# Norms computed in the stages before them: a two-block transformer step in fp32 on one core, its layers written out

## The chip, the core and the metric

The kernel runs on one core of a Trainium2 chip. A core has five engines that run their own instruction streams and meet through semaphores: TensorE (PE, matmul, with PEld for its weight loads), VectorE (DVE), ScalarE (ACT), GpSimd (POOL), and SyncE (SP), which here issues the DMAs. The metric is the device time of one execution in microseconds. One measurement of this kernel can tell about 0.2% from no change.

## The reference

256 rows of width 1024, in fp32, pass through two blocks. Cut to what matters:

```python
def first_block(x, ...):
    for layer in range(2):
        h = rmsnorm(x, g_mix); proj = h @ w_in            # 1024 x 7,756 columns
        y = sum over 3 branches of sigmoid(gate_b) * (attention_b(proj) @ w_branch[b])
        x = x + y @ w_out
        x = x + square(relu(rmsnorm(x, g_mlp) @ w_up)) @ w_down   # 1024 x 4096 and back
    return rmsnorm(x, g_final)

def second_block(x, ...):
    x = layer_norm(ALPHA * x + gated_deltanet(x), g00, b00)
    x = layer_norm(ALPHA * x + (silu(x @ w_gate) * (x @ w_up)) @ w_down, g01, b01)   # width 2816
    x = layer_norm(ALPHA * x + swa_sink_attention(x), g10, b10)
    x = layer_norm(ALPHA * x + moe_swiglu(x), g11, b11)           # 8 experts of width 3584, top 2
```

Every norm needs the mean and the variance of whole rows of x, so it cannot be finished before the last sum of the stage ahead of it.

## The kernel before

**Stages.** The kernel is a chain of stages. Each stage is one `nc.Block()`: at its end all five engines meet at a barrier, SP too. The rows of x lie in SBUF as two groups of 128 partitions (t = 0, 1), 1024 wide; a matmul needs them transposed (xT: 8 chunks of 128 partitions, 256 columns).

**Norms.** `norm_stage` is a stage of its own. DVE takes the sums of squares (`bn_stats`, two per t), a few operations on single columns and a reciprocal, ACT takes the square root, DVE scales the rows (a `tensor_scalar`, L367 or L369). PE transposes them (L397, 16 transposes into four PSUM banks), and ACT (L341, L343) and DVE (L379, L381) bring the banks to xT, multiplied by a gain (and shifted) by columns. Where the second block needs the normed x itself (final, ln00, ln01), POOL and DVE also multiply the rows with gains broadcast to all partitions (L314, L319); for ln10 this stands in the routing stage (L2463, L2465).

**Split stages.** Most products are done in three passes. ACT rounds the weights to fp32r (the "high" part), DVE subtracts to get "low", both for x (`xh`, `xl`) and for the weights, and PE sums xh·high, xl·high, xh·low. `split_projection_stage` (L550), `output_stage` (L1298) and `mlp_stage` (L1432, L1442) work so. They begin by rounding all of xT and the first two units of weights; a unit is a quarter or a half of a 2 MB tile. `projection_stage`, used for swa_proj alone, is plain fp32 (L436, L445).

**Weights.** SP loads tiles of 2 MB into a ring of six places (`Weights.load`, L198). `fill` loads the first tiles of a plan, after that each tile given free is loaded again (`load_behind`). The two layers of the first block are one body in a `Fori` loop, with a plan of its own each round; the first two tiles are loaded in the norm stage at the loop's head, the other four in a_proj. Between the layers `tidy` clears all semaphores in a stage of its own.

**Order.** First block, per layer: mix_norm, a_proj, stick-breaking attention, a_turn, bc_proj, the other branches, gates, y_turn, mix_out, mlp_norm, mlp, tidy. Second block: final norm, gdn_proj, gated delta stages, gdn_turn, gdn_out, tidy, ln00, ffn, ln01, swa_proj, sliding-window attention, swa_turn, swa_out, ln10, route, the experts (L2652, L2658; their weights pass through a ring of 1 MB places), last norm. y_turn, gdn_turn and swa_turn are stages that transpose y into xT before an output stage (L647, copies L604).

Of the kernel before, what the change touches and what calls it, by code (L numbers as in the profile page):

```python
# [64 lines left out]
BUCKETS, MAX_DIST = 32, 128  # L65
FFN_DIM, EXPERT_DIM, E = 2816, 3584, 8
# [44 lines left out]
class Core:  # L111


    def __init__(self, nc, ctx):
# [6 lines left out]
        self.scope, self.sems = ctx, []  # L121
        self.arenas = []
# [14 lines left out]
    @contextmanager  # L137
    def scratch(self, name, size=ARENA, start=0):

        outer = self.arenas  # L140
        with self.nc.sbuf_tensor(f"{name}_arena", [P, size], F32) as arena:
            self.arenas = outer + [(start, arena[:])]
            yield
        self.arenas = outer

    def sem(self, name):
        s = self.scope.enter_context(self.nc.semaphore(name))
        self.sems.append(s)
        return s

    @contextmanager
    def semaphores(self):

        outer, self.sems = (self.scope, self.sems), []
        with ExitStack() as self.scope:
            yield self.sems
        self.scope, self.sems = outer
# [22 lines left out]
class Weights:  # L180
# [3 lines left out]
    def __init__(self, core, tag, slots, plan):  # L184
        self.core, self.slots, self.plan = core, slots, plan
# [22 lines left out]
    def refill(self, sp, first, last):  # L208

        for n in range(first, last):  # L210
            if n + self.slots < len(self.plan):
                sp.wait_ge(self.tile_used, n + 1)
                self.load(sp, n + self.slots)

# [48 lines left out]
class Affine:  # L263
# [3 lines left out]
    NAMES = ("final", "ln00", "ln01", "ln10", "ln11")  # L267

    def __init__(self, core, a):
        self.core = core  # L270
        self.gain = core.sbuf("gain_columns", [P, len(self.NAMES), KC])
        self.shift = core.sbuf("shift_columns", [P, len(self.NAMES), KC])
        self.rows = core.sbuf("affine_rows", [P, 2, D])
        self.fetched = core.sem("affine_fetched")
        self.count = 0
        ln = [(a["ln_g_2"][i, j], a["ln_b_2"][i, j]) for i in range(2) for j in range(2)]
        self.sources = dict(zip(self.NAMES, [(a["g_final"], None)] + ln))

    def load_columns(self, sp, a, loaded):

        sp.dma_start(self.gain[:, 0, :], a["g_final"].rearrange("(p k) -> p k", k=KC)).then_inc(loaded, 16)
        for dst, name in ((self.gain, "ln_g_2"), (self.shift, "ln_b_2")):
            sp.dma_start(dst[:, 1:5, :], a[name].rearrange("i j (p k) -> p (i j) k", k=KC)).then_inc(loaded, 16)

    def fetch(self, sp, name):
        for i, source in enumerate(self.sources[name]):
            if source is not None:
                sp.dma_start(self.rows[:, i, :], row_broadcast(source)).then_inc(self.fetched, 16)
                self.count += 16


def norm_stage(core, tag, eps, gain, shift=None, natural=False, before=None, pool_first=None,
               vectors=None, y=None):

    nc = core.nc
    at = 0
    if y is None:  # L300
        y, at = core.part(0, NT, D)
    stats, at = core.part(at, NT, 12)
    mv, at = core.part(at, NT, 2)
    rstd, at = core.part(at, NT, 1)
    warm, at = core.part(at, 1)
    x = core.x
    rms = shift is None
    s = {n: core.sem(f"{tag}_{n}") for n in ("squares", "mean_square", "variance", "root", "inverse", "normed", "turned", "gained0", "gained1")}

    def natural_tile(eng, t):  # L310

        eng.wait_ge(core.affine.fetched, core.affine.count)
        eng.wait_ge(s["normed"], NT)
        op = eng.tensor_tensor(x[:, t, :], y[:, t, :], core.affine.rows[:, 0, :], ALU.mult)  # L314
        if not rms:
            gained = s[f"gained{t}"]
            op.then_inc(gained, 1)
            eng.wait_ge(gained, 1)
            eng.tensor_tensor(x[:, t, :], x[:, t, :], core.affine.rows[:, 1, :], ALU.add)  # L319

    with nc.Block() as block:
        @block.sync
        def _(sp):
            if before is not None:
                before(sp)

# [2645 lines left out]
```

## Time and profile before

| what | us |
|---|---|
| three runs | 2879.19, 2880.88, 2884.61 |
| median | 2880.88 |
| profiled execution: its own time | 2890.15 |
| span of its trace | 2888.4 |
| PE busy | 2598.8 (90%) |
| DVE busy | 1758.3 (61%) |
| ACT busy | 1350.9 (47%) |
| POOL busy | 110.8 (4%) |

The profile has one execution. Its windows view gives each engine's busy time in a stretch, with the clock granted to TensorE as a share of 2.4 GHz and the share of the DMA engines in use. Its waits view sums the idle time of an engine by what ended it. Its timeline lists instructions by start; a row's bracket holds the idle time ahead of it and what ended it.

### The profile page before, as it was taken

The numbers are of one execution on the slowest core, as the hardware profiler recorded it, in microseconds if no ns is written. First come the engines' busy times: TensorE is split into PE (matmuls) and PEld (weight loads), VectorE is DVE, ScalarE is ACT, GpSimd is POOL, SyncE is SP. The second block draws the span as 40 slices with busy tenths as digits, with TensorE's granted clock in tenths as the row PEclk, the third lists the DMA queues.
The fourth block names the chain that finished last, engine by engine and source line by source line (L and its number), as shares of the span: only waits on it lengthen the run. The fifth ranks groups of instructions, "written<-read, shape, count | busy, mean of one in ns | idle before, by whom it ended". The sixth has DMA issues, their size and how long they took to land. (4 is left out here: it accounts for less than half of the span.)

```text
span 2888.4 us, 34560 instructions
## 1 busy us (share of the span) xinstructions
PE 2598.8 (90%) x13577; PEld 2128.4 (74%) x13577; DVE 1758.3 (61%) x2037; ACT 1350.9 (47%) x1480; POOL 110.8 (4%) x155
## 2 busy tenths in 40 slices
PE   5999979978989799876879988799999999999996
PEld 5675469976744699746769977688887888888885
DVE  4334355543342555565554434688888988888897
ACT  3631234436312344321233413477777777777775
POOL 0100000001001000003200000000000000000000
PEclk9988989989899899887989995799999999999998
DMA  8141335162413351640055540499999999999996
GB/s 306 63 147 59 110 123 199 65 235 73 164 65 111 137 184 59 238 52 4 2 186 194 180 120 1 159 366 364 362 345 363 355 340 356 359 358 344 362 357 231
DMA packets 392739, 584.57 MB, mean 202 GB/s; under 512 B 22848, under 2 KB 286336, under 8 KB 392448
## 3 DMA queue, kind: packets, MB, share of 16 engines
q1 hardware_dynamic: 392576, 582.33, 59.3%
q8 instruction: 110, 1.80, 0.3%
q14 instruction: 53, 0.43, 0.0%
HBM read 578.09 MB, written 4.19 MB: 202 GB/s over the span
## 5 line engine op out<-in xcount | busy, mean ns | idle before, releaser
L2757 DVE TENSOR_TENSOR moe_low<-ring,moe_high 128x2048 fp32r<-128x2048 f32 x288 | 658.4, 2290 | 106.9 <-ACT moe_high L2721 101.8
L2721 ACT CAST moe_high<-ring 128x2048 fp32r<-128x2048 f32 x288 | 549.3, 1907 | 169.0 <-PE bank L2658 88.6
L2652 PE MATMUL bank<-moe_high,moe_xh 128*128 128x512 f32 x896 | 240.8, 391 | 7.9 <-PEq L2470 7.9
L2652 PE MATMUL bank<-moe_high,moe_xl 128*128 128x512 f32 x896 | 240.5, 391 | 0.0
L2652 PE MATMUL bank<-moe_low,moe_xh 128*128 128x512 f32 x896 | 240.2, 390 | 0.0
L2652 PEld LDWEIGHTS bank<-moe_high,moe_xh 128*128 128x128 f32 x896 | 168.7, 188 | 43.0 <-issue 8.1
L2652 PEld LDWEIGHTS bank<-moe_high,moe_xl 128*128 128x128 f32 x896 | 168.9, 188 | 35.0
L2652 PEld LDWEIGHTS bank<-moe_low,moe_xh 128*128 128x128 f32 x896 | 168.6, 188 | 34.9
L2658 PE MATMUL bank<-moe_high,moe_hh 128*128 128x512 f32 x448 | 128.1, 408 | 15.5 <-DVE moe_hl L2762 8.1
L1486 DVE TENSOR_TENSOR mlp_low<-upper_ring,mlp_high 128x2048 fp32r<-128x2048 f32 x36 | 82.5, 2293 | 95.5 <-ACT mlp_high L1457 95.5
L1457 ACT CAST mlp_high<-upper_ring 128x2048 fp32r<-128x2048 f32 x36 | 68.7, 1908 | 114.7 <-PE bank L1432 58.7
L2757 DVE TENSOR_TENSOR moe_low<-xT,moe_high 128x2048 fp32r<-128x2048 f32 x48 | 110.0, 2292 | 20.1 <-ACT moe_high L2721 19.0
L2658 PE MATMUL bank<-moe_high,moe_hl 128*128 128x512 f32 x448 | 121.4, 393 | 0.0
L2658 PE MATMUL bank<-moe_low,moe_hh 128*128 128x512 f32 x448 | 119.9, 390 | 0.0
L2721 ACT CAST moe_high<-xT 128x2048 fp32r<-128x2048 f32 x48 | 91.7, 1910 | 33.5 <-PE bank L2652 18.0
L689 PE MATMUL bank<-upper_ring,xT 128*128 128x512 f32 x192 | 104.5, 678 | 3.0 <-DVE lower_arena L701 3.0
L1486 DVE TENSOR_TENSOR mlp_low<-ring,mlp_high 128x2048 fp32r<-128x2048 f32 x28 | 64.0, 2292 | 68.7 <-ACT mlp_high L1457 68.7
L2658 PEld LDWEIGHTS bank<-moe_high,moe_hl 128*128 128x128 f32 x448 | 84.8, 189 | 19.3
L2658 PEld LDWEIGHTS bank<-moe_high,moe_hh 128*128 128x128 f32 x448 | 77.6, 191 | 28.3 <-ACT moe_high L2721 17.2
L2658 PEld LDWEIGHTS bank<-moe_low,moe_hh 128*128 128x128 f32 x448 | 84.3, 188 | 17.7
L689 PE MATMUL bank<-ring,xT 128*128 128x512 f32 x192 | 91.7, 622 | 2.1 <-PEq L638 2.1
L1457 ACT CAST mlp_high<-ring 128x2048 fp32r<-128x2048 f32 x28 | 53.1, 1903 | 80.0 <-PE bank L1432 57.7
(566 smaller groups left out, 4905.7 us busy)
## 6 DMA issues: line engine op xcount, KB each, us to landing
ring<-in_moe_w_gate SPq DMA_DIRECT2D x206, 512.0 KB, 5.1
ring<-in_moe_w_up SPq DMA_DIRECT2D x206, 512.0 KB, 6.5
ring<-in_moe_w_down SPq DMA_DIRECT2D x88, 1024.0 KB, 6.9
ring<-in_w_in SPq DMA_DIRECT2D x18, 2048.0 KB, 9.3
xT<-in_moe_w_down SPq DMA_DIRECT2D x25, 1024.0 KB, 7.0
upper_ring<-in_w_in SPq DMA_DIRECT2D x10, 2048.0 KB, 14.0
upper_ring<-in_w_up SPq DMA_DIRECT2D x10, 2048.0 KB, 8.2
upper_ring<-in_w_down SPq DMA_DIRECT2D x8, 2048.0 KB, 7.7
```

The costliest lines, as they stand in the source:

```text
L689: mm = pe.matmul(self.core.banks[6 + t][:], self.core.xT[:, c, t * P:(t + 1) * P], self.w.tile(self.first + j, KC, BW)[:, c, :], start=(c ...
L1457: act.copy(unit(high, u), raw(u)).then_inc(s["weight_high"], 1)
L1486: dve.tensor_tensor(unit(low, u), raw(u), unit(high, u), ALU.subtract)\
L2652: mm = pe.matmul(core.banks[i % 2][:], (xl if other_low else xh)[:, place(m), 4 * part + c, :], wt[:, c, :], start=(part == 0 and j == 0 a ...
L2658: mm = pe.matmul(core.banks[4 + half][:], (hl if other_low else hh)[:, i % 2, c, :], wt[:, c, half * BANK:(half + 1) * BANK], start=(own = ...
L2721: act.copy(unit(high, u), ring.raw(u)).then_inc(s["weight_high"], 1)
L2757: dve.tensor_tensor(unit(low, u), ring.raw(u), unit(high, u), ALU.subtract)\
```

## The change

- A norm is no longer a stage. `Norm` (a class) puts it at the end of the stage whose sums it takes: DVE adds a bank into x and takes its squares at once (`last_sums`), the t = 0 rows as soon as their last matmul is done (`first_sum`), the scaling writes the normed rows with the gain in one operation (two for a layer norm), and PE transposes them in the same block (`turn_rows`). Only the very first norm keeps a stage.
- ACT rounds the first two weight units of the next stage in that tail (`behind`, with a `Lead`).
- The next stage takes x from the PSUM banks: `Turned.high` (ACT, 512 columns each) and `Turned.low` (DVE) round from the bank. xT is written only for bc_proj and the routing (`keep`).
- Gains and shifts are rows of all partitions, fetched by SP for the next norm once the current one is done (`Norm.fetch`); their column forms and their loads at the start are gone.
- y_turn, gdn_turn and swa_turn now lie in their output stages; swa_proj is a split stage, except for the 128 columns of V.
- The layers are written out, one plan of tiles covers both, and the plan of gdn follows it. The stages of `tidy` between them are gone; POOL clears semaphores in later stages.
- The first norm stage loads six tiles (`w.fill`), not two.
- In the first unit of a stage the pass xh·low comes ahead of xl·high.
- The routing stage no longer computes rows of x; the sixth place of the experts' ring is loaded earlier, in the output stage.

```diff
-def norm_stage(core, tag, eps, gain, shift=None, natural=False, before=None, pool_first=None,
-               vectors=None, y=None):
...
+    def last_sums(self, dve, unit_used, first_units, units, first_sum, bank):
+
+        dve.wait_ge(unit_used, first_units)
+        for t in range(NT):
+            self.add(dve, t, 0, bank(t, 0))
+
+        def first():
+            dve.wait_ge(first_sum, 1)
+            return self.add(dve, 0, 1, bank(0, 1))
+
+        def second():
+            dve.wait_ge(unit_used, units)
+            return self.add(dve, 1, 1, bank(1, 1))
+        self.halves(dve, first, second)
...
+    def behind(self, act, unit_used, units, lead):
+
+        if lead is not None:
+            act.wait_ge(unit_used, units - 1)
+            lead.high(act, 0)
+            if lead.halves:
+                lead.high(act, 1)
+        self.roots(act)
+        if lead is not None and not lead.halves:
+            act.wait_ge(unit_used, units)
+            lead.high(act, 1)
...
+    def fetch(self, sp):
+        if self.following is not None:
+            sp.wait_ge(self.s["normed"], NT)
+            self.core.affine.fetch(sp, self.following)
...
+def norm_stage(core, norm, lead, before):
...
+        def _(sp):
+            before(sp)
+            norm.fetch(sp)
...
-        norm_stage(core, "mix_norm", RMS_EPS, core.layer_vectors[:, 0, 0:KC], before=lambda sp: w.fill(sp, 0, 2),
...
-            (2, "N", BW, keep_N(core, v))], before=lambda sp: w.fill(sp, 2))
...
+                    norm_stage(core, norm, lead, w.fill)
...
-                with nc.Fori(0, DEPTH) as i:
...
-    projection_stage(core, "swa_proj", w, [(first, "T", BW, with_bias(qT, bq, 0, HD ** -0.5)),
```

`Turned.high` and `Turned.low`, and the split swa_proj:

```python
    def high(self, act, b):
        act.wait_ge(self.turned, b + 1)
        act.copy(self.part(self.core.xh, b), self.banks[b][:]).then_inc(self.x_high, 1)

    def low(self, dve, b):
        dve.wait_ge(self.x_high, b + 1)
        dve.tensor_tensor(self.part(self.core.xl, b), self.banks[b][:], self.part(self.core.xh, b), ALU.subtract)\
           .then_inc(self.x_low, 1)
...
    split_projection_stage(core, "a_proj", w, [(first, "T", BW, with_bias(qT, bq, 0, HD ** -0.5)),
                                                 (first + 1, "T", BW, with_bias(qT, bq, 4, HD ** -0.5)),
                                                 (first + 2, "KV", 3 * P, keep_kv)], x, 4,
                           before=lambda sp: core.band.fetch(sp, bias))
```

**DVE at the end of mix_out in the first layer.** Before, the last add is followed by a barrier (the branch at L346 waits for it), then come the statistics of both t, then the scaling of both, and after the transposes the copies of xT and the rounding.

```order
L1328 TENSOR_TENSOR x<-bank,x 128x512 [waits mix_out_unit_used]
L1328 TENSOR_TENSOR x<-bank,x 128x512
L1261 UNCONDITIONAL_BRANCH
L346 UNCONDITIONAL_BRANCH [waits barrier_Pool_Activation_PE_DVE_SP_release]
L350 BN_STATS mlp_norm_arena<-x 128x6 x2
L353 BN_AGGR mlp_norm_arena<-mlp_norm_arena 128x2 [waits mlp_norm_squares]
L358 SCALAR_TENSOR_TENSOR mlp_norm_arena<-mlp_norm_arena 128x1 [waits mlp_norm_squares]
L361 TENSOR_SCALAR mlp_norm_arena<-mlp_norm_arena 128x1 [waits mlp_norm_mean_square]
L350 BN_STATS mlp_norm_arena<-x 128x6 x2
```

After, at the same place:

```order
L638 TENSOR_TENSOR x<-bank,x 128x512 [waits mix_out_first_sum]
L436 BN_STATS norm_small<-x 128x6 [waits mlp_norm_step]
L447 BN_AGGR norm_small<-norm_small 128x2 [waits mlp_norm_step]
L451 SCALAR_TENSOR_TENSOR norm_small<-norm_small 128x1 [waits mlp_norm_step]
L453 TENSOR_SCALAR norm_small<-norm_small 128x1 [waits mlp_norm_step]
L473 RECIPROCAL norm_small<-norm_small 128x1 [waits mlp_norm_root,affine_fetched]
L478 SCALAR_TENSOR_TENSOR xT<-x,norm_small,affine_rows 128x1024 [waits mlp_norm_step]
L638 TENSOR_TENSOR x<-bank,x 128x512 [waits mix_out_unit_used]
L436 BN_STATS norm_small<-x 128x6 [waits mlp_norm_step]
```

The rows of t = 0 are scaled ahead of the last add of t = 1; no barrier stands between add and norm.

**SP at the first norm of the program.** Before, two tiles are issued in the norm's block and the rest in a_proj's.

```order
L198 DMA ring<-in_w_in 128x8x512
L198 ISA
L198 DMA ring<-in_w_in 128x8x512
L321 UNCONDITIONAL_BRANCH
L506 UNCONDITIONAL_BRANCH [waits barrier_Pool_Activation_PE_DVE_SP_release]
L198 ISA
L198 DMA ring<-in_w_in 128x8x512
```

After:

```order
L530 UNCONDITIONAL_BRANCH [waits barrier_Pool_Activation_PE_DVE_SP_release]
L241 DMA ring<-in_w_in 128x8x512 x3
L241 DMA upper_ring<-in_w_in 128x8x512 x3
L336 DMA affine_rows<-in_g_mlp 128x1024 [waits mix_norm_normed]
L529 UNCONDITIONAL_BRANCH
L705 UNCONDITIONAL_BRANCH [waits barrier_Pool_Activation_PE_DVE_SP_release]
```

Six tiles and a gain row now stand ahead of the barrier that opens a_proj (L705).

## Rows read from the trace of the kernel before

**Rows 1.** Windows: stretch; PE, PEld, DVE, ACT, POOL busy (count); PEclk, DMA share, GB/s

```profile
402.00:414.00 12.00, 3.68 (x16) 3.28 (x16) 9.33 (x21) 5.89 (x11) 0.00 (x0) 0.58 0.00 1
...
1735.00:1797.00 62.00, 58.59 (x247) 47.26 (x245) 25.51 (x117) 23.60 (x99) 0.00 (x0) 0.58 0.00 1
...
2400.00:2870.00 470.00, 456.75 (x2100) 377.23 (x2099) 414.13 (x299) 339.02 (x283) 0.00 (x0) 1.00 1.02 349
```

**Rows 2.** Waits of PE in the experts, longest sum: total us, times, longest

```profile
PE bank L2658 <- DVE moe_hl L2762: 8.1, 4, 2.0
```

**Rows 3.** Timeline, mix_out to mlp, first layer: start, length, instruction, [idle before]

```profile
398.82 1.07 PE L1298 MATMUL bank<-mix_out_low,mix_out_xh 128*128 128x512 f32 x4
399.93 1.29 DVE L1328 TENSOR_TENSOR x<-bank,x 128x512 f32<-128x512 f32 x2 [5.45 <-PE bank L1298]
...
404.71 0.21 DVE L353 BATCH_NORM_AGGREGATE mlp_norm_arena<-mlp_norm_arena 128x2 f32<-128x12 f32 x1
...
405.48 0.75 DVE L367 TENSOR_SCALAR mlp_norm_arena<-x,mlp_norm_arena 128x1024 f32<-128x1024 f32 x1
...
414.05 2.08 PE L1432 MATMUL bank<-mlp_xh,mlp_high 128*128 128x256 f32 x8 [4.09 <-ACT mlp_high L1457]
...
420.48 1.12 PE L1432 MATMUL bank<-mlp_xh,mlp_low 128*128 128x256 f32 x8
...
421.44 1.12 PE L1432 MATMUL bank<-mlp_xh,mlp_high 128*128 128x256 f32 x8
```

**Rows 4.** Timeline, end of the first layer to a_proj of the second

```profile
595.38 1.29 DVE L1328 TENSOR_TENSOR x<-bank,x 128x512 f32<-128x512 f32 x2 [4.15 <-PE bank L1442]
...
603.16 1.29 DVE L350 BATCH_NORM_STATS2 lower_arena<-x 128x6 f32<-128x512 f32 x2 [6.49 <-issue]
...
614.84 1.50 PE L550 MATMUL bank<-a_proj_xh,a_proj_high 128*128 128x256 f32 x8 [3.24 <-ACT a_proj_high L585]
```

**Rows 5.** Timeline, second mlp to gdn_proj, with the load of a gain row

```profile
1168.80 1.29 DVE L1328 TENSOR_TENSOR x<-bank,x 128x512 f32<-128x512 f32 x2 [4.15 <-PE bank L1442]
...
1186.44 2.08 PE L550 MATMUL bank<-gdn_proj_xh,gdn_proj_high 128*128 128x256 f32 x8 [4.37 <-ACT gdn_proj_high L585]
...
1193.90 5.25 SPq L288 DMA_DIRECT2D affine_rows<-in_ln_g  x1
```

**Rows 6.** Timeline, gdn_out to ffn

```profile
1472.02 1.28 DVE L1329 SCALAR_TENSOR_TENSOR x<-x,bank 128x512 f32<-128x512 f32 x2 [5.45 <-PE bank L1298]
...
1493.47 2.08 PE L1432 MATMUL bank<-ffn_xh,ffn_high 128*128 128x256 f32 x8 [7.63 <-ACT ffn_high L1457]
```

**Rows 7.** Timeline, ffn to swa_proj

```profile
1684.45 1.29 DVE L1329 SCALAR_TENSOR_TENSOR x<-x,bank 128x512 f32<-128x512 f32 x2 [1.43 <-PE bank L1442]
...
1698.79 30.64 PE L445 MATMUL bank<-xT,upper_ring 128*128 128x256 f32 x128 [4.76 <-PEq L321]
...
1729.26 7.07 PE L445 MATMUL bank<-xT,ring 128*128 128x256 f32 x32
```

**Rows 8.** Timeline, gate to mix_out in the first layer

```profile
368.78 0.69 DVE L1229 TENSOR_TENSOR lower_arena<-bank,lower_arena 128x512 f32<-128x512 f32 x1 [2.74 <-PE bank L1202]
...
369.55 1.26 POOL L1240 TENSOR_TENSOR upper_bc_arena<-upper_bc_arena,lower_arena 128x512 f32<-128x512 f32 x1 [2.17 <-DVE lower_arena L1229]
...
371.89 0.59 ACT L604 COPY xT<-bank 128x512 f32<-128x512 f32 x1 [38.47 <-PE bank L647]
...
376.25 1.73 PE L1298 MATMUL bank<-mix_out_high,mix_out_xh 128*128 128x512 f32 x4 [3.06 <-ACT mix_out_high L1283]
```

**Rows 9.** Timeline, last norm: scaling with a row of gains

```profile
2880.04 1.28 DVE L2824 SCALAR_TENSOR_TENSOR last_arena<-x,last_arena,affine_rows 128x1024 f32<-128x1024 f32 x1
```

**Rows 10.** Timeline, start: SP issues of tiles, and a_proj's second group

```profile
20.04 10.16 SPq L198 DMA_DIRECT2D ring<-in_w_in  x3
...
30.39 8.60 SPq L198 DMA_DIRECT2D upper_ring<-in_w_in  x3
...
36.04 1.12 PE L550 MATMUL bank<-a_proj_xh,a_proj_high 128*128 128x256 f32 x8
```

More of the change, by code:

```diff
@@ L279, in load_columns @@
[L279 to L283, printed above, removed]
+        self.sources = {}
+        for i in range(DEPTH):
+            self.sources[f"mix{i}"] = (a["g_mix"][i],)
+            self.sources[f"mlp{i}"] = (a["g_mlp"][i],)
@@ L292, in norm_stage @@
-def norm_stage(core, tag, eps, gain, shift=None, natural=False, before=None, pool_first=None,
-               vectors=None, y=None):
-    nc = core.nc
[L299 to L319, printed above, removed]
+            sp.dma_start(self.rows[:, i, :], row_broadcast(source)).then_inc(self.fetched, 16)
@@ new lines, in wait, with clear, __init__, high @@
+    def wait(self, eng, name):
+        eng.wait_ge(self.fetched, self.there[name])
+def clear(pool, sems):
+    for s in sems:
+        pool.sem_clear(s)
+class Lead:
+    def __init__(self, core, w, tile, raw, halves):
+        self.core, self.w, self.tile, self.raw, self.halves = core, w, tile, raw, halves
+    def high(self, act, u):
+        self.w.wait(act, self.tile)
+        act.copy(self.core.unit(self.core.high, u, self.raw(u), self.halves), self.raw(u))
+def mlp_lead(core, w, first):
+    return Lead(core, w, first, lambda u: w.tile(first, KC, BW)[:, :, u * 2 * P:(u + 1) * 2 * P], False)
@@ new lines, in norm_stage, with _, all_squares @@
+def norm_stage(core, norm, lead, before):
+    with core.nc.Block() as block:
+        @block.sync
+        def _(sp):
+            before(sp)
+            norm.fetch(sp)
+        @block.vector
+        def _(dve):
+            def all_squares(t):
+                norm.squares(dve, t, 0)
+                return norm.squares(dve, t, 1)
+            norm.halves(dve, lambda: all_squares(0), lambda: all_squares(1))
+        @block.scalar
+        def _(act):
+            norm.roots(act)
+            for u in range(2):
+                lead.high(act, u)
+        @block.tensor
+        def _(pe):
+            norm.turn_rows(pe)
@@ L2905, in first_half, with second_block, clear_between, fill_free @@
+def second_block(core, a, r, ring, gdn, results, lower, between):
+    mid = Weights(core, "mid", SLOTS, mid_plan(a))
+    swa_first = 2 * (FFN_DIM // FB)
+    raw, z, ba = results
+    def clear_between(pool):
+        clear(pool, between)
+    with core.semaphores() as of_gdn:
         with core.scratch("gdn_upper", GDN_UPPER, GDN_LOWER), \
                 core.nc.sbuf_tensor("gdn_more", [P, SLOT], F32) as more:
-            gdn_stages(core, a, gdn, raw, z, ba, more[:])
-    def fill_free(sp):
-        for n in range(SLOTS):
-            if n not in (1, 2):
+            gdn_stages(core, a, gdn, raw, z, ba, more[:], clear_between)
+        lower.close()
+        def fill_free(sp):
+            for n in (0, 3, 4, 5):
```

928 lines of the change are left out of this document (486 added, 442 removed).

## The prediction

> **What bounds the kernel now.** I read the page's shares first, then the windows view by stage, then the timeline around every stage boundary. TensorE (PE) is busy for nine tenths of the span, and in the experts for 457 of 470 us, at full clock and with the DMA engines full [rows 1]; its longest wait there sums to 8 us [rows 2]. The change does not touch the experts, which are a third of the span, so I cost them at nothing: they are bound by PE and by weights together. What can be won lies at the boundaries. There PE has little: of the 12 us between mix_out and mlp it is busy for 3.7, and its clock falls to 0.58 of 2.4 GHz, nearly the 1.2 GHz level [rows 1]. So the view to read is the timeline from the last matmul of a stage (T0) to the first matmul of the next.
>
> **Five norm boundaries before.** With T0 as the start of the last adds, the first matmul of the next stage starts at T0 + 14.1 for mlp (399.93 to 414.05, [rows 3]; the second layer repeats it), T0 + 19.5 from the first layer to the second (595.38 to 614.84, [rows 4]), T0 + 17.6 into gdn_proj [rows 5], T0 + 21.4 into ffn [rows 6] and T0 + 14.3 into swa_proj [rows 7]. That is six places in all. The layer boundary is longer because a stage of its own clears semaphores: the norm's statistics start 6.5 us after the adds [rows 4].
>
> **The tail, step by step.** After the change t = 0 gets its last sum 12 matmuls early. Four take 0.91 us at full clock (a group of four is listed with 1.07, its end is modelled [rows 3]), so the chain of t = 0 starts at T0 - 2.7. It is: one add 0.65 and one bn_stats 0.65 (halves of the x2 rows [rows 3, 4]), five small operations of about 0.2 (the L353 row, [rows 3]) with their hand-over, 1.1 together, then the scaling. The old scaling took 0.75 [rows 3]. The new one also reads a row of gains, as L2824 does, so I take 1.28 [rows 9]. That ends at T0 + 1.0. Then t = 1: add 0.65, bn_stats 0.65, small operations 1.1, scaling 1.28: normed at about T0 + 4.7. Half of the 16 transposes are left by then, about 2.3 us with their hand-over, and the barrier takes 0.3: the next block starts at T0 + 7.3. Its first matmul needs one 512-column rounding by ACT, for which I take the 0.59 of the bank copy [rows 8]: **T0 + 8.0**. Weights are rounded by then, in ACT's idle time. A layer norm has a second two-tensor operation for each t, some of it behind waits: 2.1 more, T0 + 10.1.
>
> The scaling is the one place where the new form of an operation is dearer, and the rows show it: 1.28 for two tensors against 0.75 for one. The Trainium skill (VectorE: DVE Perf Modes, Mode 2×_2P — use both read ports for one tensor) says why: a one-tensor operation can use both read ports, a two-tensor one cannot, since the second port carries the other tensor; the trace agrees. Priced by the old row, the tail would be 1.1 us shorter at each of six places.
>
> **What each boundary gives at an unchanged clock:** mlp twice, 14.1 - 8.0 = 6.1 each; second layer 19.5 - 8.0 = 11.5; gdn_proj 17.6 - 8.0 = 9.6; ffn 21.4 - 10.1 = 11.3; swa_proj 14.3 - 10.1 = 4.2. From each I take 1.5 for the clock. PE comes back after a rest with a group of eight at 2.08 instead of 1.12 [rows 3], some 1 us lost in a group; after the change it has its transposes and then passes that wait for roundings one bank at a time, so I expect one or two such groups more. The bounds are 0 and 3. This leaves 9.2 + 10.0 + 8.1 + 9.8 + 2.7 = **39.8**.
>
> **swa_proj as a split stage.** A plain fp32 matmul has two records, so the 32 records in 7.07 us are 16 matmuls of 0.44 [rows 7]. In three passes the starts of groups of eight are 0.96 apart [rows 3], 0.36 for the same product. There are 80 such products (ten blocks of 128 columns, eight chunks): 0.08 x 80 = **6** saved, if ACT and DVE keep up; 0 if they don't. Each has one operation of 1024 columns in a block, no longer than the 1.28 of [rows 9], against PE's 2.9. A sentence of the Trainium skill would give more: by FP8 and Floating Point Precision, TensorE Precision Notes, true fp32 is four passes, so three would save a quarter, 8.8 us; the rows give 6, and the sum goes by them.
>
> **Turns inside the output stages.** Before, from the last gate operation to mix_out's first matmul are 7.5 us [rows 8]. What has to stay is POOL's 1.26 [rows 8] after DVE's 0.69, the first transposes of a bank (0.4 to 1) and one rounding from the bank 0.59. The copies to xT, a barrier, and the wait for the weight rounding (ACT 1.90 at L1283 in the block, now done while PE turns) go. I take 3.5, bounds 2 and 5: 7 for two layers. gdn_out and swa_out have the same pattern without POOL: 3.5 each, **14** in all. The routing stage starts its logits sooner by the shorter norm but copies xT first, and no longer computes rows of x: 2, bounds 0 and 6, since a choice of experts and the gather follow serially.
>
> **What it costs: the first norm.** Before, the block of the first norm issues two tiles. Now it issues six and then a row, and the barrier waits for SP. The trace has what six issues take: the issues end at 30.2 for the first three and at 39.0 for the next three [rows 10], although each needs only about 0.5 when the queue is empty. They are held, as the row load at 1193.90 is, which takes 5.25 behind six tiles [rows 5]. The start stage issues five column loads less (0.5 to 1.0 us each, some 3 together, in the timeline's first 6 us), so all this comes up to 3 earlier. SP leaves the block at 39.0 - 3 + 0.4 to 5.3, in the middle 39, and a_proj's second group, at 36.0 before [rows 10], comes about 6.5 later than 39: 45.5. I take **-10**; bounds -14, and +3 if the issues do not hold the block. Behind SP stand all five engines; nobody has other work there. At the other tails the row is issued with a slot or two of the ring outstanding and I cost it at nothing: mlp uses up 16 tiles in the 181 us from 414.05 to 595.38 [rows 3, 4], 11.3 each, and a tile of 2.1 MB lands in 6 at the 349 GB/s of [rows 1], so the queue is empty; if it is not, each costs up to 3, since the transposes cover about 2 of 5.25.
>
> **Sum.** 39.8 + 6 + 14 + 2 - 10 = 51.8. The profiled execution took 2890.15 (span 2888.4), which gives 2838; it lies 9.3 above the median. From the median 2880.88 the forecast is 2829.
>
> **Rivals.**
> (1) SP does not hold the first block. For it: one issue alone is short. Against it: rows 10 at that very place. It gives 13 more: 2816.
> (2) The clock stays up. PE's rest shrinks from 14 to 8 us, with transposes inside. Then the 1.5 at six places come back, and as much at the four output stages' starts at most 3: 9 to 12, 2818. Against it: 0.58 in a 12-us stretch [rows 1]. With (1) too, 2806.
> (3) A row load is held at every tail. For it: 5.25 at 1193.90 [rows 5]. Against it: there six tiles stood ahead. Six places x 3 = 18: 2847.
> (4) Slower than before: the clock stays near its lower level well into each stage. For it: from 1735 to 1797 PE is busy for 58.6 of 62 us and the granted clock is still 0.58 [rows 1], so being busy is not enough. Its place is the first units after six norms; a group of eight then costs 0.96 more (2.08 against 1.12, [rows 3]). It decides from 52 + 6 = 58 us more, that is ten such groups more at each of six places; it gives 2887. Against it: in mlp the second unit runs at 1.12 already, 7 us after the first matmul.
> (5) Half of the tail's gain is lost, because DVE and ACT are late with low parts: the first unit's time grows by what its start gains. 2849.
>
> **Chances.** Forecast 0.47, (1) 0.15, (2) 0.14, both 0.05, (3) 0.08, (5) 0.07, (4) 0.03, and 0.01 that it is within 0.2%. Over 0.2% is about what a measurement of this kernel can tell from no change. Faster by over 0.2% is 0.96, the same 0.01, slower 0.03. The range from 2808 to 2846 holds the forecast with its bounds, (1) and (2), and leaves out both together, (3) to (5): about 0.2.
>
> **What would show it.** The first matmul after a norm at T0 + 8 to 9 (RMS) and 10 to 11 (layer norm); scalings of 1.28; a_proj starting near 40 with SP's row load as the last thing ahead of the barrier; ten blocks of swa_proj 2.9 us apart; mix_out's first matmul 4 us after the last gate operation; the experts unchanged at some 1005 us. The forecast is wrong if the clock in the windows after the boundaries is lower than before for longer than 3 us, if a row load takes over 2 us at the tails, or if a_proj starts near 30.

## The result and the profile after

Four executions of the changed kernel took 2831.16 to 2843.19 us, median 2837.64; the kernel before, on the same chip, 2882.74 (2879.19 to 2895.30). The ratio is 0.9833, 95% interval 0.9808 to 0.9857: by the ratio 48 us faster, 41 to 55. The forecast was 52 us less, 2829 by the median of before then shown, range 2808 to 2846. Of the profiled executions it said 2838; the changed kernel's took 2839.29 (span 2837.5, before 2888.4).

The page of the changed kernel: engine, busy us (share of the span), instructions. PE works nearly as long as before (2598.8), so the 51 us that the span lost are idle time.

```profile
PE 2597.4 (92%) x13657; PEld 2120.2 (75%) x13657; DVE 1751.7 (62%) x2022; ACT 1363.3 (48%) x1501; POOL 93.3 (3%) x146
```

Where it went is read from the timelines: for each stage, the time from the first matmul of one to the first of the next, in both profiles. Every number in this table is a difference of two starts of PE rows, except that the last row ends with the end of the last matmul. The decay sums are the first matmuls of the second attention branch, behind bc_proj (L994 before, L1213 after).

| from first matmul to first matmul | before | after | gain |
|---|---|---|---|
| start of the span to a_proj, first layer | 31.6 | 44.2 | -12.7 |
| to the first layer's decay sums | 161.5 | 162.7 | -1.2 |
| decay sums to gates, first layer | 132.7 | 136.1 | -3.4 |
| gates to mix_out, first / second layer | 50.4 / 50.5 | 48.0 / 47.9 | 2.5 / 2.5 |
| mix_out to mlp | 37.8 / 37.8 | 30.9 / 30.9 | 6.9 / 6.9 |
| mlp's first matmul to its first down matmul | 24.8 / 24.8 | 26.1 / 26.0 | -1.3 / -1.3 |
| from there to a_proj of the second layer | 176.0 | 166.3 | 9.8 |
| its first three jobs, to V | 24.6 | 25.5 | -0.9 |
| second layer, V to gates | 259.8 | 259.8 | 0.0 |
| first down matmul of the second mlp to gdn_proj | 174.2 | 166.3 | 7.9 |
| gdn_proj to gdn_out | 261.9 | 254.3 | 7.6 |
| gdn_out to ffn | 45.1 | 32.2 | 13.0 |
| ffn to swa_proj | 205.3 | 203.1 | 2.2 |
| swa_proj to the softmax | 42.3 | 35.5 | 6.8 |
| softmax to swa_out | 65.1 | 62.2 | 2.9 |
| swa_out to the experts | 61.6 | 58.8 | 2.8 |
| the experts, to the last matmul | 1006.3 | 1006.4 | -0.1 |

**The tail.** The timeline of the changed kernel between mix_out and mlp in the first layer, which answers to [rows 3] (start, length, instruction, [idle before]):

```profile
413.93 1.28 DVE L478 SCALAR_TENSOR_TENSOR xT<-x,norm_small,affine_rows 128x1024 f32<-128x1024 f32 x1
415.13 0.68 DVE L638 TENSOR_TENSOR x<-bank,x 128x512 f32<-128x512 f32 x1
...
417.70 1.28 DVE L478 SCALAR_TENSOR_TENSOR xT<-x,norm_small,affine_rows 128x1024 f32<-128x1024 f32 x1
419.01 0.35 SPq L336 DMA_DIRECT2D affine_rows<-in_g_mix  x1
...
419.04 1.97 PE L385 MATMUL bank<-consts,xT 128*128 128x128 f32 x8 [2.61 <-DVE xT L478]
...
421.95 2.26 PE L1565 MATMUL bank<-chain_xh,chain_high 128*128 128x256 f32 x8 [0.94 <-ACT chain_xh L395]
...
424.01 1.91 PE L1565 MATMUL bank<-chain_xh,chain_low 128*128 128x256 f32 x8
...
425.72 1.91 PE L1565 MATMUL bank<-chain_xl,chain_high 128*128 128x256 f32 x8
...
427.42 1.48 PE L1565 MATMUL bank<-chain_xh,chain_high 128*128 128x256 f32 x8
...
428.74 1.11 PE L1565 MATMUL bank<-chain_xh,chain_low 128*128 128x256 f32 x8
```

The last group of four matmuls starts at 412.90 and is done by 413.8 (T0). The scaling is 1.28 long, as priced; the rows of t = 1 are normed at T0 + 5.2 (forecast 4.7), and the first matmul of mlp comes at T0 + 8.15 (forecast 8.0, before 14.1). The gain row costs 0.35 on SP. Then comes what the forecast took 1.5 off for: groups of eight at the lower clock (2.26, 1.91, 1.91, part of 1.48), 1.3 us more in that unit than before, by the table.

One loss does not show at a boundary. The down product of mlp (hidden rows times w_down) takes longer than before, everywhere. Here is the third run of 48 down matmuls, first in the kernel before, then in the changed one (stretch, PE, PEld, DVE, ACT, POOL busy, PEclk, DMA share, GB/s):

```profile
483.72:494.62 10.90, 10.90 (x50) 9.03 (x49) 6.39 (x5) 5.34 (x5) 0.00 (x0) 1.00 0.49 178
```

```profile
493.48:504.68 11.20, 11.20 (x50) 9.00 (x49) 6.39 (x5) 5.33 (x5) 0.00 (x0) 1.00 0.51 191
```

The clock is 1.00 in both and the DMA share is the same to 0.02, so neither explains the 0.30. From the first down matmul to the last matmul of the stage it comes to 2.3 us in each mlp (156.5 and 158.9) and 0.8 in ffn (165.1 and 165.9), 5.5 in all, which the table has inside the rows that begin at a down matmul. What causes it no run tests. The changed kernel allocates the rounded weights once for a chain of stages and not in each stage, which may matter; that is a guess.

**The start.** The timeline of the first norm's block and the head of a_proj, answering to [rows 10]:

```profile
17.04 2.62 SPq L241 DMA_DIRECT2D ring<-in_w_in  x3
...
19.70 18.14 SPq L241 DMA_DIRECT2D upper_ring<-in_w_in  x3
...
24.59 1.97 PE L385 MATMUL bank<-consts,xT 128*128 128x128 f32 x8 [1.66 <-DVE xT L478]
...
37.89 5.28 SPq L336 DMA_DIRECT2D affine_rows<-in_g_mlp  x1
...
44.24 2.26 PE L756 MATMUL bank<-chain_xh,chain_high 128*128 128x256 f32 x8 [17.68 <-ACT chain_xh L395]
...
49.56 1.11 PE L756 MATMUL bank<-chain_xh,chain_high 128*128 128x256 f32 x8
```

PE is done with the norm at 26.6 and then rests for 17.7 us. The six tile issues last from 17.0 to 37.8, the row to 43.2; the barrier opens then. The second unit of a_proj starts at 49.56, where the kernel before had 36.04 [rows 10].

**The turn inside mix_out**, answering to [rows 8]:

```profile
386.16 0.69 DVE L1448 TENSOR_TENSOR lower_arena<-bank,lower_arena 128x512 f32<-128x512 f32 x1 [2.74 <-PE bank L1421]
386.93 1.26 POOL L1459 TENSOR_TENSOR xT<-xT,lower_arena 128x512 f32<-128x512 f32 x1 [2.17 <-DVE lower_arena L1448]
...
388.52 1.90 ACT L590 CAST chain_high<-ring 128x2048 fp32r<-128x2048 f32 x1 [37.84 <-PEq L1405]
...
388.54 2.03 PE L385 MATMUL bank<-consts,xT 128*128 128x128 f32 x16 [2.42 <-PEq L1405]
...
391.05 1.15 PE L615 MATMUL bank<-chain_high,chain_xh 128*128 128x512 f32 x4 [0.48 <-ACT chain_xh L395]
```

From the last gate operation to the first matmul are 4.9 us, 7.5 before. ACT rounds the weights (1.90) ahead of the first bank of x, and that, not a bank's transposes, is what the first matmul waits for.

### The profile page after: what moved, and what is told of

Its sections match the earlier page's. It is cut to its first block and busy times, and to the rows that moved or that the text cites. A ratio compares the mean times of both kernels' runs of the same rounds, so it can differ in the third digit from the quotient of the medians.

```text
span 2837.5 us, 34393 instructions
## 1 busy us (share of the span) xinstructions
PE 2597.4 (92%) x13657; PEld 2120.2 (75%) x13657; DVE 1751.7 (62%) x2022; ACT 1363.3 (48%) x1501; POOL 93.3 (3%) x146
## 5 line engine op out<-in xcount | busy, mean ns | idle before, releaser
L1620 DVE TENSOR_TENSOR chain_low<-upper_ring,chain_high 128x2048 fp32r<-128x2048 f32 x36 | 82.5, 2292 | 97.6 <-ACT chain_high L1594 97.6
L1594 ACT CAST chain_high<-upper_ring 128x2048 fp32r<-128x2048 f32 x36 | 68.5, 1903 | 120.9 <-PE bank L1565 61.9
L1620 DVE TENSOR_TENSOR chain_low<-ring,chain_high 128x2048 fp32r<-128x2048 f32 x28 | 64.2, 2291 | 74.5 <-ACT chain_high L1594 69.8
L1050 ACT ACTIVATE upper_bc_arena<-upper_bc_arena 128x128 f32<-128x128 f32 x64 | 28.6, 447 | 130.2 <-DVE upper_bc_arena L1021 130.2
```

What stands on the lines that cost most here:

```text
L1050: op = act.activation(p[:, h % 3, a:b], z[:, h % 3, a:b], ACT.Exp, bias=minus[:, h, t:t + 1], accum_out=total[:, h, t:t + 1])
L1594: act.copy(unit(core.high, u), raw(u)).then_inc(s["weight_high"], 1)
L1620: dve.tensor_tensor(unit(core.low, u), raw(u), unit(core.high, u), ALU.subtract)\
```

## The experiments

The theory is the sum of the prediction: tails cut short each boundary by what the rows price, the first norm's block is held by SP, and the clock after a boundary takes a little back. The rivals: the start's loss lies in the transfers, the gains come from elsewhere, and the clock is what decides.

**Two tiles in the first norm's block (e1_two_tiles).**

```diff
-                    norm_stage(core, norm, lead, w.fill)
+                    norm_stage(core, norm, lead, lambda sp: w.fill(sp, 0, 2))
...
-                        (base + 2, "N", BW, keep_N(core, v))], norm, 4)
+                        (base + 2, "N", BW, keep_N(core, v))], norm, 4,
+                        before=(lambda sp: w.fill(sp, 2)) if i == 0 else None)
```

> The changed kernel, but the first norm's block issues two tiles as before, and the other four are issued at the head of a_proj. Theory (the barrier of that block waits for SP, whose six tile issues and a gain row take until 43.2 us): the block ends about 0.3 us after its last transposes, near 27, a_proj's first matmul starts near 28 instead of 44.2, and the whole is 12 to 15 us shorter than the changed kernel (some 2824), unless the third tile, which is then issued later, is late for a_proj. Rival (the block was held by the transfers themselves and a_proj would wait for its tiles anyway): a_proj's first matmul earlier, but the end of a_proj moves by less than 4 us.

Measured: 2818.2 us (2813.27 to 2819.55), ratio to the kernel before 0.9776, interval 0.976 to 0.9792, where the changed kernel has 0.9833. By the ratios that is 16 us less than the changed kernel, where 12 to 15 were expected. Its timeline at the same place:

```profile
24.47 0.34 SPq L336 DMA_DIRECT2D affine_rows<-in_g_mlp  x1
...
27.26 0.55 SPq L241 DMA_DIRECT2D ring<-in_w_in  x1
...
27.93 1.29 PE L756 MATMUL bank<-chain_xh,chain_high 128*128 128x256 f32 x4 [1.45 <-ACT chain_xh L395]
```

The row is issued in 0.34, the first matmul starts at 27.9 instead of 44.2, and from there to the decay sums are 161.1 us, 162.7 in the changed kernel: a_proj does not wait for its tiles. The block was held by the issues, a_proj does not need the other four tiles earlier, and the rival falls.

**The row alone moved out (e2_row_later).**

```diff
-                            following=f"mlp{i}" if i < DEPTH else "ln00")
+                            following=None if i == 0 else f"mlp{i}" if i < DEPTH else "ln00")
...
+                        before=(lambda sp: core.affine.fetch(sp, "mlp0")) if i == 0 else None)
```

> The changed kernel with six tiles issued in the first norm's block, but with the gain row for the next norm issued at the head of a_proj. Theory: of the 16 us for which the block is held, the row is 5.3 (37.9 to 43.2 us); a_proj's first matmul moves from 44.2 to about 39. Rival (the row waits for the same place in the queue as the sixth tile, and the barrier would be late anyway): no move over 1 us.

Measured: 2830.72 us in one run. The row stands in a_proj's block now:

```profile
32.93 5.29 SPq L241 DMA_DIRECT2D upper_ring<-in_w_in  x1
...
38.86 4.69 SPq L336 DMA_DIRECT2D affine_rows<-in_g_mlp  x1
...
39.53 2.26 PE L756 MATMUL bank<-chain_xh,chain_high 128*128 128x256 f32 x8 [12.59 <-ACT chain_xh L395]
```

The first matmul comes 4.7 us earlier, the row's share. The other 11.6 of the 16.3 are the six tiles. The row's issue is still held for 4.7 us there, and it costs nothing, because no engine waits for SP in that stage.

**swa_proj in plain fp32 again (e3_swa_fp32).**

```diff
+                    if plain:
+                        if part == 0:
+                            w.wait(pe, tile)
+                        for c in range(KC):
+                            if c == KC - 1:
+                                pe.wait_ge(s["weight_low"], m + 1)
+                            if u == 0:
+                                pe.wait_ge(x.kept(), c // 2 + 1)
+                            mm = pe.matmul(banks[part // 2][:, (part % 2) * T:(part % 2 + 1) * T],
+                                           raw(u)[:, c, :], core.xT[:, c, :], start=(c == 0), stop=(c == KC - 1))
```

> The changed kernel, but the q and k columns of swa_proj are multiplied in plain fp32 (one matmul of raw weights and xT instead of three fp32r ones); the roundings are still done and PE still waits for them, but does not use them. Theory of the prediction: 0.08 us for each of 80 products, so from the first matmul of that stage to the first of the V part 6 us more (35.4 instead of 29.4 at full clock). Rival (the pages' quarter): 8.8 us more. Second rival: the split form runs into ACT and DVE and gives nothing: 0.

Measured: 2842.40 us in one run. The stage, from its first matmul to the softmax's, takes 41.3 us instead of 35.5: 5.8 more, forecast 6. By the four passes of true fp32 in the Trainium skill (FP8 and Floating Point Precision, TensorE Precision Notes) the estimate would have been 8.8; the trace does not bear that out, since a plain fp32 product takes 0.44 here and three fp32r products 0.36.

**t = 0 summed late (e6_late_t0).**

```diff
-            dve.wait_ge(first_sum, 1)
+            dve.wait_ge(unit_used, units)
```

> The changed kernel, but the sums of t = 0 in a tail are taken only when the last matmul of the stage is done, as those of t = 1. Theory of the prediction (t = 0 starts its chain 2.7 us early and so takes it off the path): the first matmul after each of the six norms starts 2 to 2.7 us later, 12 to 16 us in all for the whole. Rival (the chain of t = 1 is bound by something else): under 1 us at each.

Measured: 2850.77 us in one run. The intervals to the first matmul grow by 2.7 (mlp, twice), 3.3 (second a_proj), 3.3 (gdn_proj), 1.8 (ffn) and 0.1 (swa_proj): 13.9 in all, inside the forecast's 12 to 16. Singly they are not all inside its 2 to 2.7: two are above it, ffn is a little below, and for swa_proj the rival's "under 1" holds. In the unit that follows, 0.6 to 1.2 of each comes back, but swa_proj loses 1.1 there. Why its first matmul hardly moves, the timeline of the changed kernel says:

```profile
1648.01 0.63 PE L1575 MATMUL bank<-chain_ffn_low,mlp_hh 128*128 128x512 f32 x2
...
1650.26 0.68 DVE L639 SCALAR_TENSOR_TENSOR x<-x,bank 128x512 f32<-128x512 f32 x1
...
1653.40 1.28 DVE L475 SCALAR_TENSOR_TENSOR x<-xT,norm_small,affine_rows 128x1024 f32<-128x1024 f32 x1
...
1660.24 2.26 PE L756 MATMUL bank<-chain_ffn_xh,chain_ffn_high 128*128 128x256 f32 x8 [0.94 <-ACT chain_ffn_xh L395]
```

The last units of ffn are short, so the four adds and statistics of DVE are the queue: the last add starts 1.6 us after the last matmul (1648.64), and the first matmul comes at T0 + 11.6 where the forecast had 10.1.

**No units rounded ahead (e7_no_lead).**

```diff
-        if lead is not None:
-            act.wait_ge(unit_used, units - 1)
-            lead.high(act, 0)
-            if lead.halves:
-                lead.high(act, 1)
+        self.lead = lead
         self.roots(act)
-        if lead is not None and not lead.halves:
-            act.wait_ge(unit_used, units)
-            lead.high(act, 1)
...
+                for u in range(2):
+                    x.lead.high(act, u)
                 for b in range(4):
                     x.high(act, b)
```

> The changed kernel, but ACT rounds the first two weight units of a stage after a norm at the head of that stage, before it rounds x, and not in the tail. Theory: ACT does 2 x 1.0 us (projections) or 2 x 1.9 us (mlp, ffn) ahead of the first rounding of x, so the first matmul comes 2 us (second layer's a_proj, gdn_proj, swa_proj) or 3.8 us later (mlp twice, ffn): 17 us in all beside the held first stage, where nothing changes but 2 us more. Rival: the roundings in the tail were in the way of the square roots, so part of it comes back, under 10 in all.

Measured: 2864.86 us in one run. Mix_out to mlp grows by 3.6 (twice), ffn by 3.5, the second a_proj and gdn_proj by 2.2 each, swa_proj by 1.9, the first a_proj by 2.0; with 0.2 to 0.6 each in the units behind, 21 in all. The forecast was 17 and 2. Nothing comes back: in the tail ACT has time for these roundings.

**Scaling with one tensor (e8_one_tensor).** The gain is left out of the RMS norms.

```diff
-            op = dve.scalar_tensor_tensor(out=self.dst[:, t, :], in0=x, scalar=rstd, in1=core.affine.rows[:, 0, :],
-                                          op0=ALU.mult, op1=ALU.mult)
+            op = dve.tensor_scalar(self.dst[:, t, :], x, rstd, None, ALU.mult)
```

> The changed kernel, but the scaling of the RMS norms' rows leaves out the gain (one tensor and the root instead of two tensors). Theory of the prediction: 0.75 instead of 1.28 for each t, both on the path, so the first matmul of mlp (twice), of the second layer's a_proj and of gdn_proj comes 1.1 us earlier each, 4 in all. Rival: t = 0 is done while PE still multiplies, so only t = 1 counts: 0.5 each, 2 in all.

Measured: 2831.42 us in one run. The first matmul comes 1.1 earlier in both mlps (forecast 1.1) and 0.8 earlier in a_proj and gdn_proj; behind it the first unit is shorter too, by 1.0 in mlp (24.99 against 26.05 to the first down matmul) and 0.3 in the projections. Together 6.3 where 4 was expected. The price of the second tensor is as forecast in mlp and 0.3 less in the projections. The rest is the clock of the first unit: mlp's third and fourth group take 1.16 and 1.12 there, 1.91 and 1.48 in the changed kernel.

**Matmuls that compute nothing in the tails (e4_warm, e5_warm_two_tiles).** The edit of e5 is shown; `done` is a bank whose sums have been taken.

```diff
+                if warm:
+                    for _ in range((12 if self.shifted else 4) if t == 0 else (3 if self.shifted else 8)):
+                        pe.matmul(self.banks[3][:] if t == 0 else done[:], self.core.xl[:, 0, 0:P],
+                                  self.part(self.core.xl, 0), start=True, stop=True)
                 pe.wait_ge(ready, t + 1)
```

> The changed kernel with matmuls added that compute nothing: in each tail PE multiplies old low parts into a bank that the transposes then write over, 4 of 512 columns before the transposes of t = 0 and 8 before those of t = 1 (12 and 3 for a layer norm), in time in which PE waited. Theory (the first units after a boundary run at the lower clock because PE rested in the tail): the first groups of eight after a boundary take 1.1 instead of 2.3, 1.9, 1.9 and 1.5, some 2.4 us less at each of six boundaries, 14 in all. Rival (the clock there is not set by what PE does in those 8 us): no difference, or 1 to 3 us slower at each where an added matmul is late.

> e1_two_tiles together with the added matmuls of e4_warm; the ones before the transposes of t = 1 now go to a bank whose sums have been taken. Theory: what each gave, added: e1's 2818 less 2 us at each of the four or five boundaries where the second or third group of eight came back to 1.1 in e4_warm (10 in all): some 2808. Rival (the difference that e4_warm showed was chance of the clock): 2818, within the spread of e1.

In e4_warm the second lot went to `self.banks[3]` too, and wrote over the turned rows of t = 0 there, so a part of x is lost for what follows; the instructions and their times are the same. It took 2834.39 us (ratio 0.9836, 0.9819 to 0.9853: that of the changed kernel). e5_warm_two_tiles took 2823.2 us (2813.83 to 2826.97), ratio 0.9774, 0.975 to 0.9797: that of e1_two_tiles. So neither gives a gain that a timing shows. The first unit of mlp in e5_warm_two_tiles:

```profile
405.46 2.27 PE L1569 MATMUL bank<-chain_xh,chain_high 128*128 128x256 f32 x8 [0.94 <-ACT chain_xh L399]
407.52 1.84 PE L1569 MATMUL bank<-chain_xh,chain_low 128*128 128x256 f32 x8
409.21 1.11 PE L1569 MATMUL bank<-chain_xl,chain_high 128*128 128x256 f32 x8
```

The third group is at 1.11 instead of 1.91, and mlp's first down matmul comes 1.1 earlier. One such group is no proof: e6_late_t0, without added matmuls and with a longer rest of PE, has the same third group:

```profile
412.33 2.26 PE L1565 MATMUL bank<-chain_xh,chain_high 128*128 128x256 f32 x8 [0.94 <-ACT chain_xh L395]
414.39 1.80 PE L1565 MATMUL bank<-chain_xh,chain_low 128*128 128x256 f32 x8
416.03 1.11 PE L1565 MATMUL bank<-chain_xl,chain_high 128*128 128x256 f32 x8
```

There the unit merely starts later. The granted clock in the 20 us behind the last matmul of the first mix_out tells the two apart. In this order, the changed kernel, e6_late_t0, e5_warm_two_tiles:

```profile
413.97:433.97 20.00, 15.15 (x92) 14.56 (x93) 12.59 (x15) 6.44 (x8) 0.00 (x0) 0.74 0.33 118
```

```profile
401.63:421.63 20.00, 13.25 (x80) 12.45 (x80) 13.63 (x20) 5.76 (x8) 0.00 (x0) 0.74 0.21 65
```

```profile
398.29:418.29 20.00, 17.91 (x121) 16.34 (x120) 14.35 (x16) 6.45 (x8) 0.00 (x0) 0.91 0.39 135
```

With the added matmuls it is 0.91 at all six boundaries, in e4 and in e5; in the changed kernel it is 0.74 or 0.83, in e6 0.74 or 0.66. So the added matmuls did raise the clock there, and over the boundaries the intervals of e5 are some 9 us shorter than those of e1. The whole is not shorter, because the stretches of attention, in the second layer from a_proj's V on, are 17 us longer in the same profile (below).

**The attention stretches.** The stretch from the decay sums to the gates has the same instructions in every kernel of this study but e11_fill_all. Here are the windows of it in the kernel before and the changed one (stretch, PE, PEld, DVE, ACT, POOL busy, PEclk, DMA share, GB/s), first of before:

```profile
193.00:326.00 133.00, 121.62 (x425) 66.63 (x426) 50.19 (x199) 23.59 (x79) 2.01 (x8) 0.86 0.21 72
774.00:899.00 125.00, 113.93 (x424) 62.92 (x424) 50.13 (x198) 23.37 (x78) 2.01 (x8) 0.91 0.21 74
```

and of after:

```profile
207.00:343.00 136.00, 124.88 (x424) 67.93 (x424) 50.09 (x198) 23.37 (x78) 2.02 (x8) 0.84 0.19 69
774.00:899.00 125.00, 114.05 (x424) 62.94 (x424) 50.02 (x199) 23.37 (x78) 2.03 (x8) 0.91 0.21 75
```

The length follows the granted clock. Over all profiles it takes one of a few values: in the first layer 132.7 (before), 136.1 (after), 128.7 (e1), 132.7 (e2), 128.8 (e4), 136.1 (e5), 125.3 (e6), 136.1 (e7); in the second 125.2 in most, 128.8 in e7, 132.7 in e4, e5 and e6. The gated delta stages, from gdn_proj's V columns to the transposes of its output, do the same: 206.6 before, 202.6 after, 206.0 in e1. What picks the value is not shown. It need not be chance alone: e4, e5 and e6 have the same long value in the second layer, and in all three the stretch ahead of it (V of a_proj to the decay sums) takes 136.7 instead of 134.5. A timing of one execution thus carries up to 11 us per layer that no edit to these instructions made. It is as large as most single terms of the sum, and it is why they were read from intervals.

**More work for PE where its clock is low (e9_fill_swa, e10_fill_swa12, e12_fill_swa8, e11_fill_all).** All on top of e1_two_tiles; n is 4, 12, 8, and 4 in every softmax stage.

```diff
                     bank = core.banks[h % 2]
+                    if sink is not None:
+                        for _ in range(n):
+                            pe.transpose(bank[:, TRI:BANK], core.const("ident"), core.const("ident"))
```

> e1_two_tiles, with four transposes of a constant added in each head of the sliding-window softmax, into columns of the score bank that nothing reads. PE runs that stage at 0.53 to 0.54 of its clock, 3.58 us a head, and is busy for 54 of 57 us. Theory (it is the low share of real matrix work that keeps the clock there): the clock rises at least in part of the stage, and the stage, 62.2 us from its first score to swa_out, gets shorter than 58. Rival (four small transposes are not enough): each costs 0.25 at the lower clock, 1 us a head, 16 us more: 78.

> As e9_fill_swa with twelve transposes a head, 1.5 us a head at full clock. Theory (activity lifts the clock): stage at full clock, 16 heads of 1.8 + 1.5 us, some 60 us; the granted clock near 1. Rival (what PE does here does not decide): 12 x 0.25 = 3 us a head more, 110 us.

> e1_two_tiles with eight transposes a head in the sliding-window softmax. With four the granted clock stayed at 0.50 and the stage took 75.1 us, with twelve it was 1.00 and the stage took 57.7, without any 62.2. Theory (twelve is more than is needed): the clock is 1.00 with eight too, and the stage is 4 x 16 transposes of 0.11 to 0.13 us shorter than with twelve, about 50 us; the whole is 12 us below e1_two_tiles, some 2806. Rival (eight is too little): the clock stays at 0.50, 62.2 + 16 x 8 x 0.21 or more, about 88 us, the whole near 2844.

The sliding-window softmax in 1675 to 1730: with none (e1_two_tiles), then with four, eight and twelve transposes a head, in this order:

```profile
1675.00:1730.00 55.00, 53.54 (x200) 42.48 (x200) 24.62 (x115) 21.59 (x97) 0.00 (x0) 0.51 0.00 1
```

```profile
1675.00:1730.00 55.00, 55.00 (x210) 42.57 (x211) 18.36 (x87) 17.02 (x76) 0.00 (x0) 0.50 0.00 0
```

```profile
1675.00:1730.00 55.00, 50.60 (x360) 41.62 (x359) 29.73 (x121) 27.86 (x105) 0.00 (x0) 0.97 0.05 17
```

```profile
1675.00:1730.00 55.00, 53.08 (x400) 44.44 (x400) 25.51 (x117) 23.67 (x99) 0.00 (x0) 1.00 0.01 1
```

From the first score to swa_out's first matmul the stage takes 62.2, 75.1, 51.1 and 57.7 us. The first head's transposes stand ahead of the first score and add 0.6, 1.0 and 1.4 to swa_proj's interval. With four the rival holds (75.1, it said 78), with eight and twelve the theory (50 and 60). e12_fill_swa8 took 2808.63 us (2803.43 to 2813.07), ratio 0.9741, interval 0.9723 to 0.9759, against e1's 0.9776 (0.976 to 0.9792): the intervals part by a hair, and the ratios put it 10 us below e1, where 12 were expected. Against e1, its profile gains 11.1 us in that stage and 3.4 in the gated delta stages, and loses 6 between a_proj and the gates of the first layer, two differences that no edit to those instructions made, and 1.0 for the first head's transposes. e9_fill_swa took 2824.36 and e10_fill_swa12 2816.77 us, one run each. e12_fill_swa8 is the fastest kernel of the study. Four transposes have a second profile, in e11_fill_all, with 75.1 again; eight and twelve have one each, so how safe eight is stays open.

> As e9_fill_swa, with the four transposes a head in all softmax stages (forgetting and sparse attention in both layers too). In the changed kernel's profile the stretch from the decay sums to the gates takes 136.1 us in the first layer and 125.2 in the second, with the same instructions. Theory (there the clock is near the edge and small differences decide): with more work on PE both take the lower value, 125 plus 16 heads x 0.5 us at full clock at most, under 132, and equal to 1 us. Rival: they still differ by several us.

Measured: 2863.76 us in one run. The stretch is 143 in both layers, equal to 0.1 us, but above both values without the transposes:

```profile
190.00:333.00 143.00, 131.91 (x488) 74.57 (x488) 50.26 (x199) 23.37 (x78) 2.01 (x8) 0.85 0.19 66
767.00:910.00 143.00, 131.95 (x488) 74.61 (x488) 50.13 (x198) 23.38 (x78) 2.01 (x8) 0.85 0.19 66
```

So half of that theory fell: the layers agree, but the clock (0.85) did not rise, and the added work is paid: PE is busy for 131.9 us, 7 more than in the longest stretch without it (124.9).

## Why the prediction was right, and where its terms were off

**The boundaries.** Forecast 9.2 for the two mlps, 10.0, 8.1, 9.8, and 2.7 + 6 for swa_proj, 45.8 in all. Measured, with the first unit: 11.2 (6.9 - 1.3, twice), 8.9, 8.2, 13.2, and 8.8, 50.3. The table takes these apart. T0 is here the end of the last matmul's row, up to 0.2 later than above.

| boundary | T0 to first matmul, before | after | gain | forecast at an unchanged clock | first unit behind it |
|---|---|---|---|---|---|
| mlp, each | 14.2 | 8.0 | 6.2 | 6.1 | -1.3 |
| a_proj, second layer | 19.5 | 7.4 | 12.1 | 11.5 | -0.9 |
| gdn_proj | 17.7 | 7.4 | 10.3 | 9.6 | +0.3 |
| ffn | 21.5 | 10.0 | 11.5 | 11.3 | +0.3 |
| swa_proj | 14.4 | 11.6 | 2.8 | 4.2 | with the split form 6.8 |

So the tails themselves gave 49.0 where the sum had 48.8, and the mechanism is shown by parts: t = 0 early is worth what it was priced at in all (e6), the rounding ahead too (e7), the gain as a second tensor costs about what it was priced at (e8), the split form of swa_proj gives 5.8 of 6 (e3). swa_proj's tail is 1.4 later than forecast for a reason that the sum did not have: DVE's queue of adds and statistics behind short last units.

Three terms beside the tails were mis-sized, and they hide each other:

- The clock behind a boundary was put at 1.5 off for each of six, 9 in all. The first units lost 2.9 in the first five; swa_proj's stage gained 6.8, 1.0 more than its split form explains.
- The output stages' own matmuls were put at nothing, and gained 2.9: mix_out's 96 take 22.9 us instead of 23.6, twice, and gdn_out's 22.1 instead of 23.6. They now follow their own transposes, and run at once at full clock: the granted clock in the 2 us from mix_out's first matmul is 1.00, 0.59 before.
- The down products were put at nothing, and lost the 5.5 of "The tail" above.

49.0 - 2.9 + 6.8 + 2.9 - 5.5 = 50.3.

**The turns.** Forecast 3.5 for each of four; measured 2.5 and 2.5 in mix_out, 3.3 in gdn_out (the transposes come 20.1 earlier, the first matmul 23.4), 2.9 in swa_out with its softmax. The step that failed is "now done while PE turns": the weight rounding of 1.90 does lie beside the transposes, but ahead of x's first bank on ACT's queue, and so stays on the path: the first matmul waits for x's first rounding, which starts at 390.32, as that of the weights ends.

**The start.** Forecast -10, bound -14. At the place for which that was worked out, the second unit of a_proj, it cost 13.5 (36.04 and 49.56), and 13.9 by the decay sums. e1 and e2 show the mechanism, and its split into 11.6 and 4.7 of 16.3. SP left the block at 43.2 instead of 39: the row took 5.28, where the middle of its bounds (0.4 to 5.3) was taken, and the six tiles were done at 37.8, not at 36. The 6.5 from there to the second unit were right (6.4).

**Routing.** 2 forecast, 2.8 measured, of which 0.8 is the shorter run of matmuls in swa_out. **The experts** did not move: 1006.3 and 1006.4.

**The rivals.** (1) is excluded by the start. (2), the clock staying up, did not come as it was told, since the groups behind a boundary are at 2.26, 1.91, 1.91. But in size much of it came: the first units lost far less than 9, and the output stages' starts gave the 3 that it named. The down products' loss hid that. (3) is excluded by 0.35 at the tails. (4) and (5) have a small true part, the 1.3 us in mlp's first unit.

**The sum.** Measured terms: 50.3 + 5.0 + 6.2 + 2.8 - 13.9 = 50.4 of the 50.9 by which the last matmul moved. What is left, 0.5, is mostly the difference of two stretches that nobody forecast: 3.4 lost in the first layer's attention and 4.0 won in the gated delta stages. That the forecast for the profiled execution was met to 1 us is thus in good part luck: boundaries and routing 5 too low, turns 3 too high, the start's loss 4 too small, and inside the boundaries a clock term 7 too dear and 2.9 gained for nothing against 5.5 lost in the down products.

## What to carry to other kernels

A barrier that includes the engine that issues DMAs waits for its issues, and here these were held for over 5 us each when several 2 MB transfers were outstanding. Put loads that are needed later behind the barrier, at the head of a stage in which nobody waits for that engine. A norm that needs the last sum can have all but half a chain taken off the path by splitting its rows by when their sums are ready. When edits are worth 1 to 10 us and the clock of latency-bound stretches moves by as much, read them as intervals between the same instructions of two traces, not as a difference of two timings.

## What the runs showed of the hardware

- SP's issue of a 2 MB tile took 0.5 us with an empty queue and over 5 us (5.29) behind several; a gain row took 0.34 to 0.35 alone and 5.28 behind six tiles.
- Fuller use of PE made a stage shorter: eight transposes that compute nothing in each head moved the granted clock from 0.51 to 0.97 and the stage from 62.2 to 51.1 us; four left it at 0.50 and cost 13 us. PE was busy for 53.5 of 55 us at 0.51 already. The Trainium skill (TensorE: Matmul & The Clock Gate, Part 1: The HAM clock gate (the "warmup" mystery)) says that activity releases the throttle; the runs agree in so far as added work raised the clock.
- The same instructions in attention took 125.2, 128.7, 132.7 or 136.1 us, with a granted clock from 0.91 (125.2) to 0.84 (136.1).
- Matmuls that compute nothing, added where PE waits in a tail, raised the granted clock of the next 20 us from 0.74 to 0.91 and shortened the boundaries by some 9 us; no timing of the whole shows a gain.
- The same 48 down matmuls took 10.90 us in one kernel and 11.20 in the other at a granted clock of 1.00 and a DMA share of 0.5. The cause is open.
